# Attention steps: VectorE copies the finished tile's sums out of PSUM, and ScalarE runs its first exponential ahead of roots, table loads, norm and transfers

## What is computed

```python
def diff_core(q, k, v, mask, lam):
    s = jnp.einsum('bqhmd,bkhmd->bhmqk', q, k) * (DA_DK ** -0.5)
    if mask is not None:
        s = jnp.where(mask, s, jnp.finfo(jnp.float32).min)
    p = jax.nn.softmax(s, axis=-1)
    a = p[:, :, 0] - lam * p[:, :, 1]
    return jnp.einsum('bhqk,bkhe->bqhe', a.astype(v.dtype), v)

dq = rope(rms_norm(dq, lp['g_qn']), pos)
dk = rope(rms_norm(dk, lp['g_kn']), pos)
o_d = rms_norm(diff_core(dq, dk, dv, ...), lp['g_dnorm']) * (1.0 - lam_init)
```

## Time and profile before

| | us |
|---|---|
| median of 3 runs | 2238.75 |
| lowest and highest | 2237.01, 2238.88 |
| the profiled execution's own time | 2238.77 |
| its span, first to last instruction | 2237.0 |
| attention stage in the span | about 490 to 1080 |

### The profile page before, as it was taken

One profiled execution on the slowest core, in us unless ns is written; L12 is line 12 of the kernel. 1 busy time (PEld: TensorE's weight loads), 2 busy tenths in 40 slices (PEclk: granted clock), 3 DMA queues, 4 the chain that ended last, 5 costly groups with the idle time before them and its releaser, 6 DMA issues.

```text
span 2237.0 us, 34167 instructions
## 1 busy us (share of the span) xinstructions
PE 2221.1 (99%) x13160; PEld 2090.7 (93%) x13160; DVE 1076.9 (48%) x2032; ACT 655.3 (29%) x1519; POOL 666.8 (30%) x368
## 2 busy tenths in 40 slices
PE   8999999999999999999999999999999999999999
PEld 8999777789898898998999999999999999999999
DVE  5312444445535455355145558666666663313432
ACT  5200333335535445354212122111101104334311
POOL 4522210230130400401350534222333325576520
PEclk9999999999999999999999999999999999999999
DMA  7622222230130310302951322222222126656311
GB/s 254 199 91 76 71 69 87 77 103 27 31 109 27 103 42 25 118 24 63 313 177 54 115 65 76 76 67 76 66 66 76 60 67 202 186 162 203 98 50 49
DMA packets 312667, 218.18 MB, mean 98 GB/s; under 512 B 16331, under 2 KB 303678, under 8 KB 312543
## 3 DMA queue, kind: packets, MB, share of 16 engines
q1 hardware_dynamic: 219802, 117.33, 18.1%
q10 hardware_dynamic: 92740, 99.15, 13.2%
HBM read 160.15 MB, written 56.29 MB: 97 GB/s over the span
## 4 chain that ended last, share of the span: by engine, by line
PE 95%; ACT 3%; issue 1%; DVE 1%; ACTq 0%; DMA 0%; DVEq 0%
PE ps L606 28%; PE ps L608 28%; PE ps L607 28%; PE ps L846 3%; PE ps L873 2%; PE ps L796 1%; PE ps L801 1%; PE ps L1011 1%; PE ps L798 1%; PE ps L864 1%; ACT L1442 1%; ACT L1393 1%; ACT full L1386 0%; PE ps L849 0%; ACT scr L1442 0%
## 5 line engine op out<-in xcount | busy, mean ns | idle before, releaser
L606 PE MATMUL ps<-a_hi,w_hi 128*128 128x352 f32 x2920 | 946.9, 324 | 0.0
L607 PE MATMUL ps<-a_lo,w_hi 128*128 128x352 f32 x2920 | 935.9, 321 | 0.0
L608 PE MATMUL ps<-a_hi,w_lo 128*128 128x352 f32 x2920 | 935.9, 321 | 0.0
L504 POOL TENSOR_SCALAR w_hi<-w_raw 128x1024 fp32r<-128x1024 f32 x150 | 163.5, 1090 | 1431.2 <-PE ps L608 872.9
L606 PEld LDWEIGHTS ps<-a_hi,w_hi 128*128 128x128 f32 x2920 | 547.8, 188 | 3.6 <-issue 2.9
L607 PEld LDWEIGHTS ps<-a_lo,w_hi 128*128 128x128 f32 x2920 | 548.7, 188 | 0.4
L608 PEld LDWEIGHTS ps<-a_hi,w_lo 128*128 128x128 f32 x2920 | 547.9, 188 | 0.0
L506 POOL TENSOR_TENSOR w_lo<-w_raw,w_hi 128x1024 fp32r<-128x1024 f32 x150 | 363.9, 2426 | 12.5
L606 PE MATMUL ps<-w_hi,a_hi 128*128 128x384 f32 (+3 forms) x864 | 318.6, 369 | 0.0
L608 PE MATMUL ps<-w_hi,a_lo 128*128 128x384 f32 (+3 forms) x864 | 307.6, 356 | 0.0
L607 PE MATMUL ps<-w_lo,a_hi 128*128 128x384 f32 (+3 forms) x864 | 306.6, 355 | 0.0
(11 more groups left out here) (212 smaller groups left out, 2298.1 us busy)
## 6 DMA issues: line engine op xcount, KB each, us to landing
w_raw<-w_in SPq DMA_DIRECT2D x64, 512.0 KB, 4.3
w_raw<-w_down SPq DMA_DIRECT2D x48, 512.0 KB, 3.8
w_raw<-w_up SPq DMA_DIRECT2D x44, 512.0 KB, 3.8
hid_d<-scr ACTq DMA_DIRECT2D x22, 512.0 KB, 2.6
w_raw<-w_down SPq DMA_DIRECT2D x24, 384.0 KB, 3.3
scr<-gates_d ACTq DMA_DIRECT2D x24, 352.0 KB, 6.5
gates_d<-full ACTq DMA_DIRECT2D x13, 528.0 KB, 2.6
xt_d<-full ACTq DMA_DIRECT2D x1, 4224.0 KB
```

Of the source, the lines that this page charges most:

```text
L504: pool.tensor_scalar(hi, raw, 1.0, 0.0, ALU.mult, ALU.add).then_inc(S["w_hi_done"], 1)
L606: pe.matmul(out, lhs[0], rhs[0], start=start, stop=False)
L607: pe.matmul(out, lhs[0], rhs[1], start=False, stop=False)
L608: return pe.matmul(out, lhs[1], rhs[0], start=False, stop=stop)
```

## The change

VectorE now copies a finished tile's sums out of bank 7 into `o_n` at the start of a step, once ScalarE has taken their square sum, and TensorE's next use of the bank waits for that copy (`inv_ev`, which stands at 3 when the stage begins). ScalarE writes its squares to the other buffer of `o_n` and norms the sums in place in SBUF. ScalarE's order in a step becomes: square of the sums, copy of v, two copies of the stored tile, four squares of q and k, first exponential, root for q and k, root for the sums, norm of the sums, transfer of v, transfer to `o_d`, transfer of k, second exponential. VectorE takes the inverse of the sums' root after that of q and k, or after their place where a step has no turned tile.

```diff
--- before.py
+++ after.py
@@ -972,7 +972,7 @@
                     if n == 0:
                         pe.wait_ge(S["state_done"], RET_TILES)
                     else:
-                        pe.wait_ge(S["do_nrm"], n)
+                        pe.wait_ge(S["inv_ev"], 3 + n)
                     if n >= 2:
                         pe.wait_ge(S["dot_ev"], 2 * (n - 1))
                     last = weigh_v(i, 0, min(4, every))
@@ -1367,37 +1367,12 @@
                     act.wait_ge(S["pv_done"], n + 1)
                     if n >= 1:
                         act.wait_ge(S["dot_tr"], n)
-                    act.activation(o_n[0:r, b, :], ps[0:r, 7, 0:DV], ACT.Square,
+                    act.activation(o_n[0:r, 1 - b, :], ps[0:r, 7, 0:DV], ACT.Square,
                                    accum_out=st[0:r, b:b + 1]).then_inc(S["do_sq"], 1)
                 if turned:
                     h, i, n = turned
                     r, b = rows(i), i % 2
-                    act.wait_ge(S["pa_done"], n + 1)
-                    if n == 0:
-                        act.wait_ge(S["rope_done"], 2 * RET_TILES)
-                    else:
-                        act.wait_ge(S["d_rope"], 2 * n)
-                    if i == 0 and h:
-                        act.wait_ge(part_st[1], h * 48)
-                    for m in range(4):
-                        if m == 3:
-                            act.wait_ge(S["pb_done"], n + 1)
-                        bank, at = (2 * b, m * P) if m < 3 else (2 * b + 1, 0)
-                        act.activation(nrm[0:r, m * P:(m + 1) * P], ps[0:r, bank, at:at + P], ACT.Square,
-                                       accum_out=st[0:r, 8 + 4 * b + m:9 + 4 * b + m]).then_inc(S["d_sq"], 1)
-                if normed:
-                    h, i, n = normed
-                    r, b = rows(i), i % 2
-                    act.wait_ge(S["do_sq"], n + 1)
-                    act.wait_ge(S["r_eps"], n + 1)
-                    act.activation(st[0:r, 2 + b:3 + b], st[0:r, b:b + 1], ACT.Sqrt, bias=eps_sum(i, r),
-                                   scale=1.0 / DV).then_inc(S["do_rt"], 1)
-                if turned:
-                    h, i, n = turned
-                    r, b = rows(i), i % 2
-                    act.wait_ge(S["d_sq"], 4 * (n + 1))
-                    act.activation(st[0:r, 16 + 4 * b:20 + 4 * b], st[0:r, 8 + 4 * b:12 + 4 * b], ACT.Sqrt,
-                                   bias=tok_eps[0:r, i:i + 1], scale=1.0 / DK).then_inc(S["d_rt"], 1)
+                    act.wait_ge(S["pb_done"], n + 1)
                     if n == 0:
                         act.wait_ge(S["kv_done"], RET_TILES)
                     if i == 0 and h:
@@ -1405,19 +1380,12 @@
                         act.wait_ge(S["v_st"], h * (16 * TILES))
                     act.activation(v_tok[0:r, i, :], ps[0:r, 2 * b + 1, P:3 * P], ACT.Copy,
                                    scale=tok_inv[0:r, i:i + 1]).then_inc(S["d_v"], 1)
-                    act.wait_ge(S["d_v"], n + 1)
-                    out = t["new_v_prompt"][0, 0, i * P:(i + 1) * P] if i < LAST else t["new_v_sample"][0, 0]
-                    act.dma_start(out[:, h:h + 1].rearrange("t h d -> t (h d)"), v_tok[0:r, i, :]).then_inc(S["v_st"], 16)
-                if normed:
-                    h, i, n = normed
-                    r, b = rows(i), i % 2
-                    act.wait_ge(S["do_inv"], n + 1)
-                    act.activation(o_n[0:r, b, :], ps[0:r, 7, 0:DV], ACT.Copy,
-                                   scale=st[0:r, 4 + b:5 + b]).then_inc(S["do_nrm"], 1)
                 if stored:
                     h, i, n = stored
                     r, b = rows(i), i % 2
                     act.wait_ge(S["dot_tr"], n + 1)
+                    if normed:
+                        act.wait_ge(S["inv_ev"], 3 + normed[2] + 1)
                     if n == 0:
                         act.wait_ge(ot_st[0], RET_TILES // 2 * 16)
                         act.wait_ge(ot_st[1], RET_TILES // 2 * 16)
@@ -1426,9 +1394,19 @@
                     for m in range(2):
                         act.activation(o_t[:, b, m, 0:r], ps[:, 7, (2 + m) * P:(2 + m) * P + r], ACT.Copy,
                                        scale=cols[:, 24 + m:25 + m]).then_inc(S["dot_ev"], 1)
-                    act.wait_ge(S["dot_ev"], 2 * (n + 1))
-                    act.dma_start(o_d[2 * h:2 * h + 2, :, i * P:i * P + r].rearrange("m p n -> p m n"),
-                                  o_t[:, b, :, 0:r]).then_inc(dot_st[b], 16)
+                if turned:
+                    h, i, n = turned
+                    r, b = rows(i), i % 2
+                    if n == 0:
+                        act.wait_ge(S["rope_done"], 2 * RET_TILES)
+                    else:
+                        act.wait_ge(S["d_rope"], 2 * n)
+                    if i == 0 and h:
+                        act.wait_ge(part_st[1], h * 48)
+                    for m in range(4):
+                        bank, at = (2 * b, m * P) if m < 3 else (2 * b + 1, 0)
+                        act.activation(nrm[0:r, m * P:(m + 1) * P], ps[0:r, bank, at:at + P], ACT.Square,
+                                       accum_out=st[0:r, 8 + 4 * b + m:9 + 4 * b + m]).then_inc(S["d_sq"], 1)
                 if scored:
                     h, i, n = scored
                     r, b = rows(i), i % 2
@@ -1441,6 +1419,34 @@
                         act.wait_ge(S["a_done"], n)
                     act.activation(e0[0:r, 0:keys], score_rows(0, i), ACT.Exp, bias=st[0:r, 24 + b:25 + b],
                                    accum_out=st[0:r, 28 + 2 * b:29 + 2 * b]).then_inc(S["e0_done"], 1)
+                if turned:
+                    h, i, n = turned
+                    r, b = rows(i), i % 2
+                    act.wait_ge(S["d_sq"], 4 * (n + 1))
+                    act.activation(st[0:r, 16 + 4 * b:20 + 4 * b], st[0:r, 8 + 4 * b:12 + 4 * b], ACT.Sqrt,
+                                   bias=tok_eps[0:r, i:i + 1], scale=1.0 / DK).then_inc(S["d_rt"], 1)
+                if normed:
+                    h, i, n = normed
+                    r, b = rows(i), i % 2
+                    act.wait_ge(S["do_sq"], n + 1)
+                    act.wait_ge(S["r_eps"], n + 1)
+                    act.activation(st[0:r, 2 + b:3 + b], st[0:r, b:b + 1], ACT.Sqrt, bias=eps_sum(i, r),
+                                   scale=1.0 / DV).then_inc(S["do_rt"], 1)
+                    act.wait_ge(S["do_inv"], n + 1)
+                    act.activation(o_n[0:r, b, :], o_n[0:r, b, :], ACT.Copy,
+                                   scale=st[0:r, 4 + b:5 + b]).then_inc(S["do_nrm"], 1)
+                if turned:
+                    h, i, n = turned
+                    r, b = rows(i), i % 2
+                    act.wait_ge(S["d_v"], n + 1)
+                    out = t["new_v_prompt"][0, 0, i * P:(i + 1) * P] if i < LAST else t["new_v_sample"][0, 0]
+                    act.dma_start(out[:, h:h + 1].rearrange("t h d -> t (h d)"), v_tok[0:r, i, :]).then_inc(S["v_st"], 16)
+                if stored:
+                    h, i, n = stored
+                    r, b = rows(i), i % 2
+                    act.wait_ge(S["dot_ev"], 2 * (n + 1))
+                    act.dma_start(o_d[2 * h:2 * h + 2, :, i * P:i * P + r].rearrange("m p n -> p m n"),
+                                  o_t[:, b, :, 0:r]).then_inc(dot_st[b], 16)
                 if turned:
                     h, i, n = turned
                     r, b = rows(i), i % 2
@@ -1862,14 +1868,20 @@
 
             dve.wait_ge(S["g_scaled"], 2)
             dve.wait_ge(S["lam_d"], 1)
+            def inverse_of_sum(h, i, n):
+
+                r, b = rows(i), i % 2
+                dve.wait_ge(S["do_rt"], n + 1)
+                dve.reciprocal(st[0:r, 4 + b:5 + b], st[0:r, 2 + b:3 + b]).then_inc(S["do_inv"], 1)
+
             for s in range(DIFF_STEPS):
                 turned, scored, weighed, normed = (tile_at(s, lag) for lag in range(1, 5))
                 fill = fill_at(s, 1)
                 if normed:
                     h, i, n = normed
                     r, b = rows(i), i % 2
-                    dve.wait_ge(S["do_rt"], n + 1)
-                    dve.reciprocal(st[0:r, 4 + b:5 + b], st[0:r, 2 + b:3 + b]).then_inc(S["do_inv"], 1)
+                    dve.wait_ge(S["do_sq"], n + 1)
+                    dve.tensor_copy(o_n[0:r, b, :], ps[0:r, 7, 0:DV]).then_inc(S["inv_ev"], 1)
                 if fill:
                     h, k = fill
                     for n in (2 * k, 2 * k + 1):
@@ -1905,6 +1917,8 @@
                     r, b = rows(i), i % 2
                     dve.wait_ge(S["d_rt"], n + 1)
                     dve.reciprocal(st[0:r, 36 + 4 * b:40 + 4 * b], st[0:r, 16 + 4 * b:20 + 4 * b]).then_inc(S["d_inv"], 1)
+                    if normed:
+                        inverse_of_sum(*normed)
                     dve.wait_ge(S["d_inv"], n + 1)
                     if i == 0 and h:
                         dve.wait_ge(part_st[0], h * 48)
```

(2 more changed lines are left out.)

## The result

| | before | changed |
|---|---|---|
| median of 20 runs, us | 2238.73 | 2242.43 |
| lowest, highest | 2236.68, 2241.31 | 2240.90, 2244.80 |
| span of the profiled execution | 2237.0 | 2243.0 |

The ratio is 1.0019, with a 95% interval from 1.0012 to 1.0025: slower by 3.7 us, and inside the 0.2% that I had called no change. The forecast was 2243.0.

The account below looks back on a forecast made before the run. TensorE, busy 99% of the span, was taken to bound the kernel. From 2238.77 us, -4.1 for stalls removed at `scores(1)` and +8.4 for new waits before `scores(0)` gave 2243.0, range 2235.5 to 2248.5.

Parts of the forecast that it names:

- What could be won: TensorE's stalls at `scores(1)` of long tiles: 3.1 us of loss plus 1.0 of restarts, at most about 4.1 us.
- The nine waits: TensorE's waits for ScalarE's first exponential at `scores(1)` of the long tiles; all nine should go.
- The copy for nothing: VectorE's 36 copies of about 0.42 us lie beside matmuls and cost nothing; uncovered, up to 0.42 in one step.
- The chain: First exponential through root, rope, second exponential to q and k copies, before the next `scores(0)`: 10.52 us against 9.79, tile 0.
- Where the second load stands: ScalarE's second table load stands behind the k transfer, not behind the second maximum; a switch costs 1.29 us.
- Tile 0 alone still needs a table load before it: Load before the first exponential in each head's first scored step; 0.12 us of it on the chain.
- The sum: Profiled execution 2238.77 us, -4.1 gain and +8.4 cost, +4.3 together: 2243.0.
- 0.49 against 0.48: Chances of the whole outcome: same (within 4.5 us) 0.49, slower 0.48; faster had 0.03.
- The load behind the second maximum: Rival: the second table load waits for the second maximum; cost +12.0, time 2246.7 us; chance 0.15.
- the copies that do not bind: Rival: the late q and k copies do not delay `scores(0)`, only the gain is left, 2234.7 us; chance 0.12.
- the third: Rival: first exponential no earlier where it matters, old stalls stay and new ones come, 2247.2 us; chance 0.06.
- The price of a table switch: ScalarE's table load priced at 1.29 us from the rows, against the skill's 2.66 with a drain of 1.38.

Follow-up runs that it names:

- e1_roots_first: Changed kernel with both roots (q and k, then the sums) put back ahead of the first exponential: 2233.72 us against 2237.98 before, ratio 0.9978.
- e4_copy_alone: Kernel before with VectorE's copy of the sums and the norm in SBUF, ScalarE's order as before: 2239.32 us, ratio 1.0003.
- e2_k_transfer_behind: Changed kernel with the transfer of k moved behind the second exponential: 2235.20 us, ratio 0.9987.
- e3_copies_first: Changed kernel with VectorE's copies of q and k ahead of the ratio and weighting of the same step: 2235.68 us, ratio 0.9987.
- e7_extra_copy: Changed kernel with VectorE's copy of q made twice in each step: 2249.26 us, ratio 1.0050.
- e8_change_again: The changed kernel, unaltered, profiled a second time: one execution, 2241.01 us, span 2239.2.
- e5_order_alone: Changed kernel without VectorE's copy; the norm reads bank 7 and TensorE waits for it before weighing v: 2289.67 us, ratio 1.0231.

## Why the prediction was right

- **What could be won.** The mechanism was right, the size a little low: forecast 4.1 us at most, measured 4.7 by intervals, the same in the changed kernel and in `e1_roots_first` (4.3 in medians). The nine waits and their restarts come to 4.2. The other 0.6 was lost at tile 6's `scores(1)` in the last three heads, which the earlier trace rows does not list.
- **The copy for nothing.** Right to 0.15 us: `e4_copy_alone`.
- **The chain.** Forecast 10.52, measured 10.48 for tile 0; waits forecast 0.73, 0.42, 0.05 and 0.47, measured 0.69, 0.41, nearly nothing before tile 3, and 0.39. Its parts bear it out one by one: the k transfer and the load behind it (`e2_k_transfer_behind`), the queue on VectorE (`e3_copies_first`), the missing slack (`e7_extra_copy`), the place of the roots (`e1_roots_first`).
- **Where the second load stands.** Right for all 36 second exponentials, which wait for one thing alone (`e2_k_transfer_behind`). It was wrong for the one first exponential that I took to be like the others: "Tile 0 alone still needs a table load before it" was priced at 0.12 in all four heads. In the first its load waits for the maximum and puts 1.2 us more on the chain. This was in the trace of before as well, where the same load followed the same maximum by 0.10 us (I read another head's).
- **The sum.** 2243.0 against 2242.43, and that it is so near is in part luck. The cost was forecast at 8.4 us and measured 8.4 by intervals (in `e8_change_again`), but of other parts: 0.69 + 0.52 + 0.13 + 0.39 a head and 0.07 in tile 3's scores are 7.2 us in all, and the first head's load, which I did not have, added 1.2. The gain was 4.7 and not 4.1, and -4.7 + 8.4 is the 3.7 measured. Whether the time would stay inside the bound of 4.5 us that I had called no change was close to a toss by my own chances, 0.49 against 0.48.
- **The rivals.** The load behind the second maximum and the copies that do not bind are both out. So is the third: TensorE's wait at `scores(1)` is gone in every long tile.
- The price of a table switch: the root above starts 1.29 us after its load did, and in `e1_roots_first` 697.60 - 696.30 = 1.30. The Trainium skill (ScalarE: Activation LUTs, What ACT_TABLE_LOAD costs) has 2.66 with a drain; no run here shows the drain. The Trainium skill (ScalarE: Activation LUTs, Rules for kernel authors) asks to do all of one table set before switching. By that, `e1_roots_first` is the better order, and it is the faster one; but 2.66 us a switch is not the reason. A root between two exponentials puts a load behind it, and here the k transfer held that load on the chain: `e2_k_transfer_behind` keeps the root in between and the waits are nearly gone.

## What to carry to other kernels

Before an instruction is put ahead of others, follow what now stands behind it to the next thing that the bound engine asks for, and compare that chain with the engine's own interval, for the shortest tile too: here the long tiles had the waits to win, and the short ones had no slack to pay with. Move only what has to move: norm and transfers were enough, and the roots, whose results others wait for, belonged in front. An independent transfer that waits for a late result must not stand ahead of a table load or an activation that others wait for.

## What the hardware showed that I had not expected

- A table load began before the waits of its activation were over when these were two (maximum and weighting) or one, and it waited for the maximum when there were three. Moving two of them brought it forward by its own length, 1.28 us. Both of those were waits for transfers, so whether their number or their kind decides is not shown.
- The times of some small VectorE instructions look as if GpSimd held them. In the 32-row tile of the first head, VectorE and GpSimd in the first profile of the changed kernel:

```profile
618.60 1.97 DVE L1960 SCALAR_TENSOR_TENSOR scr<-scr,eps 32x1 f32<-32x1 f32 x1
620.50 1.07 DVE L1962 SCALAR_TENSOR_TENSOR scr<-scr,lamt 32x1 f32<-32x1 f32 x1
621.61 2.57 DVE L1971 SCALAR_TENSOR_TENSOR scr<-scr 32x160 f32<-32x160 f32 x1
```

```profile
618.17 2.38 POOL L506 TENSOR_TENSOR w_lo<-w_raw,w_hi 128x1024 fp32r<-128x1024 f32 x1
620.53 1.04 POOL L504 TENSOR_SCALAR w_hi<-w_raw 128x1024 fp32r<-128x1024 f32 x1
621.65 2.35 POOL L506 TENSOR_TENSOR w_lo<-w_raw,w_hi 128x1024 fp32r<-128x1024 f32 x1
```

  The first two end with the GpSimd instruction that they overlap, the third 0.18 us after it. The first two do so within 0.02 us in all heads of both profiles of the changed kernel, with one exception that speaks for the same reading: in the last head no GpSimd instruction follows the first, and the second takes 0.20 instead of 1.07. The third was held this once; where it takes 0.37, in the second and third head and in `e8_change_again`, it starts just as closely ahead of a GpSimd instruction, by 0.05 us (0.04 here). What made the difference is open. They read and write SBUF alone; copies out of PSUM in the same stretch keep their times. This made the wait of 0.81. That the two engines exclude each other there is my reading of the times, not tested.
- A long wait can be followed by a lower clock of TensorE, but need not be. Two stretches of `e5_order_alone`, with the wait of 2.68 us in the first head and with the same wait in the second, and one of `e7_extra_copy`, behind the wait of 2.04 us, each with the granted clock third from the end:

```profile
609.00:617.00 8.00, 7.01 (x25) 5.14 (x26) 4.63 (x12) 1.94 (x3) 0.00 (x0) 0.79 0.09 25
769.00:777.00 8.00, 7.15 (x37) 5.96 (x38) 5.53 (x16) 3.01 (x5) 0.00 (x0) 1.00 0.09 27
```

```profile
513.00:517.00 4.00, 3.92 (x14) 3.80 (x15) 0.65 (x3) 2.15 (x4) 0.00 (x0) 0.57 0.10 33
```

  Part of the first and the third stretch ran at the lower level of 1.2 GHz, the second at full clock throughout. In the third and fourth head of `e5_order_alone` the clock fell again (0.81 over 927 to 936 us, 0.79 over 1087 to 1095). Behind its waits of 2.00 us it stayed at 1.00 in all four heads. The waits of 1.59 us and less in the changed kernel were followed by no fall; its clock stays at 1.00 through the stage. So the length of the wait alone does not decide, and what else does was not tested.
